# Expert 0's rows by one-hot products, later row gathers, expert weights in 4 KB runs, columns taken two apart

## The reference

```python
def hierarchical_moe(h, rg_w, rg_b, re_w, re_b, w_gate, w_up, w_down):
    p_group = softmax(h @ rg_w + rg_b)                 # 4 groups, top 1
    g_prob, g_idx = lax.top_k(p_group, 1)
    e_logits = (h @ re_w + re_b).reshape(-1, 4, 4)     # 4 experts in each group
    sel = take the chosen group's row
    top_p, top_i = lax.top_k(softmax(sel), 2)          # top 2 in the group
    w = g_prob * top_p / sum(top_p)
    for e in range(16):
        y = (silu(h @ w_gate[e]) * (h @ w_up[e])) @ w_down[e]
        out = out + combine[:, e:e + 1] * y
```

## Time and profile before

| | |
|---|---|
| median of three runs | 552.17 us (551.52 to 552.62) |
| the profiled execution | 552.4 us |
| its span, first to last instruction | 550.6 us |
| TensorE busy | 98% of the span |
| VectorE busy | 77% |
| ScalarE busy | 64% |
| GpSimd busy | 17% |
| mean granted TensorE clock | 0.996 of full |

### The profile page before, as it was taken

How to read it: one execution, slowest core, us unless ns; L and a number is a source line. 1 busy time by engine, 2 the same in 40 slices (tenths; PEclk the granted TensorE clock), 3 DMA queues, 4 the chain that set the end, 5 groups by cost and what they waited for, 6 DMA issues and landing times.

```text
span 550.6 us, 7873 instructions
## 1 busy us (share of the span) xinstructions
PE 536.9 (98%) x2662; PEld 438.5 (80%) x2663; DVE 421.3 (77%) x580; ACT 353.3 (64%) x470; POOL 91.3 (17%) x113
## 2 busy tenths in 40 slices
PE   7999999999999999999999999999999999999995
PEld 5988777777877888877788888888888888888883
DVE  5654599554864753588989898988989898988986
ACT  5563654780326253355778978788778978788745
POOL 3260000000000000031412222022212222110420
PEclk9999999999999999999999999999999999999998
DMA  8999122323020237639999999999999999999796
GB/s 322 371 283 401 42 71 77 76 79 77 0 77 0 78 114 251 234 138 313 349 380 373 379 394 382 367 371 376 392 352 374 375 390 373 376 390 393 251 208 212
DMA packets 63821, 144.03 MB, mean 262 GB/s; under 512 B 3833, under 2 KB 13361, under 8 KB 63665
## 3 DMA queue, kind: packets, MB, share of 16 engines
q1 hardware_dynamic: 56528, 120.24, 61.4%
q0 software_dynamic: 7120, 22.90, 13.7%
q10 hardware_dynamic: 144, 0.52, 0.3%
HBM read 132.77 MB, written 14.30 MB: 267 GB/s over the span
## 4 chain that ended last, share of the span: by engine, by line
PE 88%; DVE 5%; ACT 2%; DMA 2%; issue 1%; POOL 0%; DVEq 0%; POOLq 0%
PE ps L1495 25%; PE ps L1497 24%; PE ps L1496 24%; PE ps L1502 7%; PE ps L1646 2%; PE ps L1632 2%; PE ps L1608 1%; PE ps L1578 1%; PE ps L1673 1%; DMA arena<-h_dram,meta 1%; DMA arena<-norm_g 1%; DVE lo_ring L1305 1%; DVE act_lo L1015 1%; PE ps L1896 1%; DVE res L1474 0%
## 5 line engine op out<-in xcount | busy, mean ns | idle before, releaser
L1305 DVE TENSOR_TENSOR lo_ring<-arena,hi_ring 128x2048 fp32r<-128x2048 f32 x94 | 213.8, 2288 | 26.9 <-ACT hi_ring L894 26.8
L1495 PE MATMUL ps<-hi_ring,act_hi 128*128 128x512 f32 x576 | 229.8, 399 | 1.5 <-DVE lo_ring L1305 1.1
L1497 PE MATMUL ps<-hi_ring,act_lo 128*128 128x512 f32 x576 | 224.9, 390 | 0.0
L1496 PE MATMUL ps<-lo_ring,act_hi 128*128 128x512 f32 x576 | 224.4, 390 | 0.0
L894 ACT ACTIVATE hi_ring<-arena 128x2048 fp32r<-128x2048 f32 x94 | 180.2, 1917 | 28.1 <-PE ps L1497 28.1
L1495 PEld LDWEIGHTS ps<-hi_ring,act_hi 128*128 128x128 f32 x576 | 108.3, 188 | 23.5 <-issue 2.4
L1497 PEld LDWEIGHTS ps<-hi_ring,act_lo 128*128 128x128 f32 x576 | 108.1, 188 | 23.3
L1496 PEld LDWEIGHTS ps<-lo_ring,act_hi 128*128 128x128 f32 x576 | 108.4, 188 | 20.9
L1005 DVE SCALAR_TENSOR_TENSOR lo_ring<-arena,over,hi_ring 128x512 fp32r<-128x512 f32 x40 | 29.2, 747 | 29.4 <-ACT hi_ring L708 29.2
L1015 DVE TENSOR_TENSOR act_lo<-ps,act_hi 128x512 fp32r<-128x512 f32 x56 | 36.7, 683 | 7.6 <-ACT act_hi L742 5.6
L600 POOL DMA_INDIRECT arena<-h_dram,gather_idx x14 | 34.7, 2478 | 24.0 <-issue 24.0
(11 more groups left out here) (237 smaller groups left out, 523.0 us busy)
## 6 DMA issues: line engine op xcount, KB each, us to landing
arena<-w_gate SPq DMA_DIRECT2D x32, 1024.0 KB, 16.6
arena<-w_up SPq DMA_DIRECT2D x32, 1024.0 KB, 17.6
arena<-w_down SPq DMA_DIRECT2D x32, 1024.0 KB, 15.2
arena<-w_in SPq DMA_DIRECT2D x16, 512.0 KB, 7.2
y_dram<-arena POOLq DMA_DIRECT2D x8, 512.0 KB, 11.2
res<-y_dram POOLq DMA_DIRECT2D x8, 512.0 KB, 9.8
arena<-w_in SPq DMA_DIRECT2D x2, 1024.0 KB, 10.9
arena<-w_out SPq DMA_DIRECT2D x4, 512.0 KB, 6.5
```

Source lines behind the costliest of these rows:

```text
L1305: nc.vector.tensor_tensor(lo(N1 + n12), raw(n12), hi(N1 + n12).bitcast(F32), ALU.subtract).then_inc(lo_done, 1)
L1495: nc.tensor.matmul(dst, a_hi, b_hi, start=start, stop=False)
L1496: nc.tensor.matmul(dst, a_hi, b_lo, start=False, stop=False)
L1497: return nc.tensor.matmul(dst, a_lo, b_hi, start=False, stop=stop)
```

## The change

Four things are changed together.

1. Expert 0's transposed rows are no longer gathered. VectorE makes a one-hot matrix `first_hot` for each token tile (token against its place in expert 0's list), and TensorE multiplies the normed rows with it (`first_rows`, 32 matmuls of 128x128 into banks 4 and 5). For that all four tiles of normed rows stay in SBUF (`h2_home`, two of them in the raw arena's slots 9 and 10). The junk products are gone.
2. The lists of all experts are made after the first product of expert 0, and the weights of the tokens are worked out ahead of them; the difference of the logits that they need moves to GpSimd. Experts 1, 2 and 3 are gathered whole (128 places), with row numbers straight from `meta`. VectorE's work on lengths, slots and flags moves into its steps 0 and 1.
3. SyncE's load of slot 8 waits for the last store of normed rows; those of slots 9 and 10 wait for the one-hot products.
4. Gate and up weights are read in runs of 4 KB, two rows of the matrix at a time. A weight tile then holds even or odd rows, so the rows' columns are taken with a step of two (`row_cols`), in the one-hot products and in every transpose of rows. The two result buffers `y0` and `y1` change places.

```diff
-            keep_clock(3, 0)
+            def row_cols(a, i):
+                c0 = 4 * a * P + i // 2 * 2 * P + i % 2
+                return slice(c0, c0 + 2 * P - 1, 2)
+
+            def first_rows(t, a):
+                pe.wait_ge(h2_ready, t + 1)
+                pe.wait_ge(first_hot_set, t + 1)
+                for i in range(4):
+                    ins = nc.tensor.matmul(ps[:, 4 + a, i * P:(i + 1) * P], h2_home[t][:, row_cols(a, i)],
+                                           first_hot[:, t, :], start=(t == 0 and i == 0), stop=(t == T - 1 and i == 3),
+                                           skip_group_check=True)
+                return ins
+
+            first_rows(0, 0)
             logits(2 * T - 1)
-            keep_clock(2, 0)
+            first_rows(0, 1)
+            first_rows(1, 0)
...
-            keep_clock(21, 0)
+            first_rows(1, 1)
+            for a in range(2):
+                first_rows(2, a)
+                first_rows(3, a).then_inc(x_turned, 1)
...
-                    turn(4 + a, [x_rows[b][:, (4 * a + i) * P:(4 * a + i + 1) * P] for i in range(4)]
+                    turn(4 + a, [x_rows[b][:, row_cols(a, i)] for i in range(4)]
...
-            pe.wait_ge(rows_in[0], 16)
-            for a in range(2):
-                turn(4 + a, [x_rows[0][:, (4 * a + i) * P:(4 * a + i + 1) * P] for i in range(4)]).then_inc(x_turned, 1)
+            pe.wait_ge(x_lo, 1)
+            product(0, xt[0], 0, 0, 0, True, False, first=True)
+            pe.wait_ge(index_ready, 4)
+            for t in range(T):
+                pe.wait_ge(onehot_ready, t + 1)
+                ins = list_fields(7, 0, t, t == 0, t == T - 1)
+            ins.then_inc(lists_made, 1)
+            pe.wait_ge(x_lo, 2)
+            product(0, xt[0], 4, 1, 1, False, True)
```

```diff
-        w_gate_v = w_gate.rearrange("a e (k p) n -> (a e) p k n", p=P)
+        w_gate_v = w_gate.rearrange("a e (h g p j) n -> (a e) p h g (j n)", h=2, g=2, p=P)
...
-                if n == RING2 - 4:
-                    sp.wait_ge(rows_in[0], 16)
+                if n == O_BIAS // GRAN - 1:
+                    sp.wait_ge(h2_out[T - 1], 16)
+                elif n == O_BIAS // GRAN:
+                    sp.wait_ge(x_turned, 1)
+                elif n == O_BIAS // GRAN + 1:
+                    sp.wait_ge(x_turned, 2)
...
             pool.wait_ge(lists_ready, 1)
+            pool.wait_ge(x_turned, 2)
...
+            gather_whole(1)
+            gather_whole(2)
```

More of the change, by code:

```diff
@@ L894, in split, with rows_hi @@
                 nc.scalar.activation(hi(N1 + n12), raw(n12), ACT.Copy).then_inc(hi_done, 1)
-            def rows_hi(b, wait):
-                for a in range(2):
+            def rows_hi(b, wait, halves=range(2)):
+                for a in halves:
                     act.wait_ge(x_turned, wait + a)
@@ L1339, in _ @@
+            rows_lo(0, 1, (0,))
+            for piece in range(2):
+                split_piece(N1 + 1, piece)
+            rows_lo(0, 1, (1,))
+            for piece in range(2, 4):
+                split_piece(N1 + 1, piece)
             dve.wait_ge(gate_e, 1)
@@ L1379, in _, with set_lengths @@
[L1379 to L1382 removed]
+            def set_lengths():
+                step_done(nc.vector.tensor_scalar(quarters, count, float(QUARTER), None, ALU.is_gt))
+                for i in (2, 3):
+                    step_done(nc.vector.scalar_tensor_tensor(quarters, count, float(QUARTER * i), quarters,
+                                                             ALU.is_gt, ALU.add))
+                nc.vector.tensor_copy(meta_v[:, :, 3:4], quarters.unsqueeze(2)).then_inc(lengths_made, 1)
@@ L1383, in step @@
+            def step(b, e, last=False, first=False):
                 for c in range(PER_E):
                     split(e * PER_E + 4 + c, (4 + PER_E * b + c) % RING2)
+                    if first and c == 0 and b == 0:
+                        rows_lo(1, 3)
+                    if first and c == 4 and b == 0:
+                        set_slots()
+                    if first and c == 5 and b == 0:
+                        set_flags()
+                    if first and c == 0 and b:
+                        sum_flags((1, 2, 4))
+                    if first and c == 2 and b:
+                        sum_flags((8, 16, 32))
+                        nc.vector.tensor_copy(over[:, UNITS + 1:2 * UNITS + 1], flags[0]).then_inc(over_set, 1)
@@ L1390, in step @@
                         row_lo(hid_t[1], 6, hid_t[0], hid_hi, e + 1, hid_lo)
+                        if first and b == 0:
+                            set_lengths()
                     if c == 3 and not last:
                         rows_lo(b, e * 2 + 5)
-            split(3, 3)
-            rows_lo(1, 3)
-            with dve.Fori(0, E // 2 - 1) as q:
+            for e in range(2):
+                step(e, e, first=True)
+            with dve.Fori(1, E // 2 - 1) as q:
                 for b in range(2):
```

219 lines of the change are left out of this document (111 added, 108 removed).

## The result

The changed kernel takes 556.45 us (median of 17 runs, 554.86 to 559.71), beside 552.53 us for the kernel before (17 runs, 551.52 to 555.69) on the same chips. The ratio is 1.0067 with a 95% interval of 1.0052 to 1.0082: 3.9 us slower. The forecast was 554.0 us; its range ended at 556.0, so the measured median lies 0.45 us outside of it.

A forecast was written before the change was run, and what follows sets the result against it. TensorE's own work bounds the steady state; the joint before expert 0 can be shortened. Terms -0.2 - 1.1 + 2.0 = +0.7, with the clock's 1.3 +2.0 on 552.2: 554.2, rounded down to 554.0 us; range 549.6 to 556.0.

The forecast's parts named there:

- the lead of expert 0: Start of expert 0: first product 6.4 us earlier (244.6 against 251.04), a lead of 4.3 us at expert 1's transposes.
- the clock: Step 0, TensorE's wait for expert 1's rows: clock falls from 2.4 to 1.2 GHz, +1.3 us (bounds nothing and 6.3).
- transposes of expert 1's rows against before: Step 0: after a wait of 4.1 us for the gather, transposes come at 259.1 instead of 259.34, -0.2 us.
- VectorE's old wait of 1.13: First step: TensorE's wait of 1.13 us for VectorE's cut of n = 4 goes, -1.1 us.
- VectorE's moved work, steps 0 and 1: Steps 0 and 1: small work added to VectorE makes TensorE wait 2.0 us in all (bounds nothing and 4.5).
- step of two: Transposes' operand in each of 14 experts: the strided read costs nothing (bounds nothing and 11 us).
- A float32 matmul of 128 columns takes (183.23 - 181.09) / 20 = 0.107 us: One-hot matmuls ahead of expert 0: 0.107 us each, sixteen of 32 behind the last tiles, halves ready at 242.8 and 243.7.
- The landing: Gather of expert 1: starts at 250.4, lands 8.7 us later among weight loads, rows in at 259.1.
- The surplus on VectorE: Steps 0 and 1: VectorE's work exceeds TensorE's by some 1.4 us, giving TensorE waits of 2.0 us in all.
- The lead survives: Rival, 20%: expert 1's gather starts earlier or lands in 4.9 to 6.4 us, wait 0.3 to 1.8, 549.8 us.
- The gather is later than any before: Rival, 10%: 4 KB runs delay expert 1's gather by 1.6 us more; with the clock 555.6 us.
- The kept clock: Rival, 30%: same wait for expert 1's rows, but the clock does not fall, 552.9 us.

The follow-up runs named there:

- experiment 5: The changed kernel with the eight one-hot matmuls of the third token tile left out: 555.79 us, ratio 1.0050.
- experiment 3: The changed kernel with SyncE's weight loads from n = 10, 12 or 14 on held until expert 1's rows are in: 551.14, 551.94 and 556.16 us.
- experiment 6: The kernel with early lists, VectorE's sums of flags moved behind the cuts of the third and fifth slot: 550.71 us, ratio 0.9971.
- experiment 1: The changed kernel with 18 junk products filling TensorE's idle time ahead of the transposes of expert 1's rows: 554.55 us, ratio 1.0026.
- early lists: The changed kernel with lists made between the last one-hot products and written right behind VectorE's first low part: 550.8 us, ratio 0.9963; again 551.27 us.
- the hold from n = 10: The changed kernel with SyncE's weight loads from n = 10 on waiting until expert 1's rows are in: 551.14 us, ratio 0.9966.

## Why the forecast was right in kind and 2.5 us low

The direction, the place and the chain were right: the lead of expert 0 is spent on a wait for expert 1's rows, the clock falls in it, VectorE's work comes back in steps 0 and 1. Part 3 of the change and the exchange of y0 and y1 were not undone by any run. Term by term, on the axes of the two profiled runs:

| term | forecast | measured |
|---|---|---|
| transposes of expert 1's rows against before | -0.2 | +1.43 |
| VectorE's old wait of 1.13 | -1.1 | -1.13 |
| VectorE's moved work, steps 0 and 1 | +2.0 | +0.85 |
| the clock | +1.3 | +1.5 |
| step of two (13 steps) | 0 | +0.7 |
| sum | +2.0 | +3.4 |

At the hidden values of expert 14 the two runs are 3.39 us apart (514.64 and 518.03), TensorE's last matmul ends 3.19 us later, and the span is 3.7 us longer; the last 0.5 arises behind TensorE's work and was not looked into. The medians differ by 3.9. The first term is 1.6 us too low and the third 1.2 too high: without that second error the forecast would have been further off.

**The step that failed is the first: "A float32 matmul of 128 columns takes (183.23 - 181.09) / 20 = 0.107 us".** The view counts records, and such a matmul leaves two. It could have been seen in the code, for the loop behind the row of x20 makes ten matmuls (1 + 2 + 3 + 4), and forty over its four calls, where the trace of the kernel before has 80 records:

```python
for t in range(T):
    for kt in range(t + 1):
        ins = nc.tensor.matmul(ps[:, RET_BANKS[i], t * P:(t + 1) * P], scm[:, c:c + P],
```

```profile
L1646 PE MATMUL ps<-arena x80: 270/275/347, 132.1 to 183.2; 128*128 128x128 f32 x80
```

So the earlier trace rows gives 0.214 us, and the row of x40 after is the 20 matmuls behind the ranks, 0.235 us each (241.50 to 246.21). A transpose leaves one record. By the page FP8 and Floating Point Precision of the Trainium skill, section TensorE Precision Notes, a true float32 product needs four passes. The trace agrees: the products' matmuls of 512 columns in the faster format follow each other at 0.23 us, a quarter of the columns at four passes is the same 0.23.

Also, 20 matmuls stand behind the ranks and not 16. On the way to the gather the price counts as a wait: VectorE stands idle for 0.64 us ahead of its first low part, because ScalarE's high part comes late behind the matmuls. With eight of them left out (experiment 5) this wait is gone and the gather starts 0.8 us earlier. The wait is half of what the low part is late (ready at 245.84 instead of 244.55); 0.3 more is the choice, which came later than forecast, and the rest VectorE's own small work. The forecast's sum also has a slip of 0.2: 249.5 + 0.19 + 0.9 is 250.6 and not 250.4. So the gather starts 1.4 us later than forecast, it lands 0.3 slower, and the rows are in at 260.77 instead of 259.1: the term of -0.2 became +1.43. TensorE itself comes 1.5 us later too (256.5 for 255.0), through its own 20 matmuls, so the wait has the size forecast, 4.2 for 4.1, while all of it stands later. That is luck: a right number of a wait is no proof of the times at its ends.

**The landing** was taken as a fixed 8.7 us. It is not fixed: experiment 3 shows 5.5 us on idle DMA engines and 8.9 with two more pairs of weight loads ahead. That it came out near 8.7 here is presumably because the backlog is alike, which no run measures.

**The surplus on VectorE** was priced at 2.0 and costs 0.85; the mechanism is shown by experiment 6, only the size was off. The 0.85 is what the steps between the hidden values of experts 0, 1 and 2 take (18.53 and 17.79 us) above the 17.73 of a later step. With the clock kept (experiment 1) it is 18.86 and 17.79, so 1.2: a part of the surplus hides in the slow stretch. I let each piece delay the next cut and did not count that VectorE stands idle from 257.7 to 262.2, waiting with everyone else for expert 1's rows. That this makes the difference is not shown: with early lists, where this wait is gone, the surplus is 1.2 as well.

**The step of two** was put at nothing from a row without such a read, the misread 0.107 us again; this is the second step that failed. It costs 0.01 us a transpose. By the page SBUF — State Buffer of the Trainium skill, section Door 1: The DMA port swizzle, two hits in a line of 16 bytes give full bandwidth, and by it the step would be free. The transposes' row shows 1.12 us against 1.04, so the measurement decides against it, if only for 8%.

**The rivals.** "The lead survives" did not come, but it is what the kernels with early lists and with the hold from n = 10 are: its bound, a landing below 7 us or an earlier gather, was right, and its 549.8 us close to their 550.8 and 551.1. "The gather is later than any before" is refuted in its cause: the landing is the same with runs of 2 and 4 KB (9.06 and 9.0 us). The kept clock did not come of itself; experiment 1 makes it, at 554.55 us where the rival had 552.9.

## What to carry to other kernels

When a stage is made to start earlier, ask what the stage behind it waits for and whether its transfer starts earlier as well: here nothing was gained until the lists went ahead too. Here a gather landed late behind weight loads already issued, and holding two pairs of them back won as much (551.1 us) as starting it earlier (550.8); loads issued behind it did no harm. Before a duration is divided by a count in a view, hold that count against the loop in the code.

## What was not expected of the hardware

The clock does not fall at a fixed time. With TensorE's work ended at about 256.5 it went down in the microsecond behind 258 in one run of the changed kernel, and only in that behind 261, after the first transposes had begun, in another; in both it was back within the microsecond behind 265. Waits of 0.7, 0.9 and 1.7 us left it at 1.00, those of 4.1 us and more never did, and no wait between the two was seen. Windows of the first of these two runs:

```profile
258.00:259.00 1.00, 0.00 (x0) 0.00 (x0) 0.00 (x0) 0.00 (x0) 0.00 (x0) 0.84 1.01 393
259.00:260.00 1.00, 0.00 (x0) 0.00 (x0) 0.00 (x0) 0.00 (x0) 0.00 (x0) 0.50 1.02 402
```

The issue of a whole gather by GpSimd takes 2.19 us where VectorE cuts slots of 2048 columns (251.78) and 1.12 us where it does small pieces (247.91, early lists). No run parts the two causes that are left, VectorE's work and the place in the program.
